# Fifteen gather slots instead of twelve, with memory taken from the descriptor ring and the queries, and two pieces of ScalarE work moved, in a hybrid encoder kernel

## The reference, cut to what matters

```
q = (yt @ w_q).reshape(T, 8, 2, 128)
s = einsum('thpc,pnc->thpn', q, sub_keys)
val, idx = top_k(s, 16)
cand = val[:, :, 0, :, None] + val[:, :, 1, None, :]
top_val, top_pos = top_k(cand.reshape(T, 8, 256), 16)
gate = softmax(top_val)
act = gate * gelu(einsum('thkd,td->thk', u[expert], yt))
out = einsum('thk,thkd->td', act, v[expert])
```

## Time and profile before

| | |
|---|---|
| three runs | 1624.79, 1625.91 (median) and 1631.22 us |
| the profiled execution | 1626.37 us, of which the span of its instructions is 1624.6 us |
| busy share of the span | PE 64%, PEld 44%, DVE 69%, ACT 28%, POOL 31% |
| moved by DMA | 649.84 MB, on average 400 GB/s; 553.68 MB of it by the gathers |

### The profile page before, as it was taken

How to read it: one execution, slowest core, us unless ns; L and a number is a source line. 1 busy time by engine, 2 the same in 40 slices (tenths; PEclk the granted TensorE clock), 3 DMA queues, 4 the chain that set the end, 5 groups by cost and what they waited for, 6 DMA issues and landing times.

```text
span 1624.6 us, 19989 instructions
## 1 busy us (share of the span) xinstructions
PE 1046.7 (64%) x6936; PEld 712.2 (44%) x6936; DVE 1113.1 (69%) x3119; ACT 462.3 (28%) x953; POOL 502.6 (31%) x541
## 2 busy tenths in 40 slices
PE   8996876747644476867573477776576444544454
PEld 8995643525411265756451165655364111211111
DVE  3446768675577765987756765897756777777764
ACT  4101544111011235743121134763222111111110
POOL 0012334322233322333313322332323333333330
PEclk9997868868855799888796579887897566666655
DMA  9969999999999999899999999899999999999994
GB/s 371 355 230 380 417 411 408 419 421 417 418 422 421 421 418 417 352 421 407 420 416 421 421 419 417 353 409 394 415 418 405 422 422 422 421 422 422 421 421 194
DMA packets 106164, 649.84 MB, mean 400 GB/s; under 512 B 11728, under 2 KB 15824, under 8 KB 38480
## 3 DMA queue, kind: packets, MB, share of 16 engines
q0 software_dynamic: 76032, 553.68, 82.4%
q1 hardware_dynamic: 26400, 92.81, 14.7%
q10 hardware_dynamic: 3632, 2.08, 0.4%
HBM read 647.48 MB, written 1.05 MB: 399 GB/s over the span
## 4 chain that ended last, share of the span: by engine, by line
DMA 40%; PE 26%; DVE 16%; POOL 5%; ACT 5%; issue 5%; DVEq 2%; POOLq 0%; ACTq 0%
DMA ring<-in_uv_dram,expert 33%; PE ps L668 13%; DMA wring<-in_wall_dram 8%; DVE ring L1197 7%; PE ps L845 7%; POOL ring L391 5%; ACT side L569 2%; PE ps L858 2%; DVE side L1252 2%; PE ps L675 1%; ACT L460 1%; PE ps L833 1%; DVE picked L1189 1%; DVE mix L1213 1%; PE ps L886 1%
## 5 line engine op out<-in xcount | busy, mean ns | idle before, releaser
L1197 DVE CUSTOM_DVE_ANT_0 ring<-ring,ps 128x1024 f32<-128x1024 f32 x528 | 635.2, 1219 | 321.2 <-DMA ring<-in_uv_dram,expert 250.8
L391 POOL DMA_INDIRECT ring<-in_uv_dram,expert x528 | 500.5, 948 | 1086.6 <-PE ps L845 840.0
L845 PE MATMUL ps<-ring,mix 128*32 128x512 f32 x2112 | 365.6, 827 | 311.4 <-DVE mix L1213 311.2
L845 PEld LDWEIGHTS ps<-ring,mix 128*32 128x32 f32 x2112 | 67.4, 134 | 509.7 <-DVE mix L1213 367.8
L668 PE MATMUL ps<-yT,wring 128*128 128x128 f32 (+1 forms) x1472 | 205.6, 301 | 71.8 <-DMA wring<-in_wall_dram 43.7
L642 ACT ACTIVATE gel<-dots 128x4 f32<-128x4 f32 x132 | 27.1, 205 | 739.2 <-DVE dots L1197 738.8
L668 PEld LDWEIGHTS ps<-yT,wring 128*128 128x128 f32 x1472 | 193.6, 207 | 94.6 <-DMA wring<-in_wall_dram 48.1
L858 PE MATMUL ps<-sel,osb 128*128 128x16 f32 x528 | 84.0, 304 | 78.6 <-ACT osb L628 78.6
L858 PEld LDWEIGHTS ps<-sel,osb 128*128 128x128 f32 x528 | 80.6, 241 | 116.7 <-ACT osb L628 116.7
L569 ACT ACTIVATE side<-ident,params 128x128 f32<-128x128 f32 x310 | 96.5, 389 | 16.0 <-PE ps L886 14.8
L833 PE MATMUL ps<-ident,yg 128*128 128x128 f32 x264 | 49.1, 348 | 71.6 <-DVE dots L1197 71.6
(11 more groups left out here) (207 smaller groups left out, 1043.8 us busy)
## 6 DMA issues: line engine op xcount, KB each, us to landing
wring<-in_wall_dram SPq DMA_DIRECT2D x124, 512.0 KB, 12.2
ring<-in_wall_dram SPq DMA_DIRECT2D x52, 512.0 KB, 13.2
ring<-in_uv_dram,expert POOLq DMA_INDIRECT x528, 16.3
out_dram<-fo ACTq DMA_DIRECT2D x16, 64.0 KB, 6.9
hT<-in_xT_dram ACTq DMA_DIRECT2D x1, 576.0 KB, 15.9
hT<-in_xT_dram SPq DMA_DIRECT2D x2, 256.0 KB, 3.3
params<-in_smalls_dram ACTq DMA_DIRECT2D x1, 380.0 KB, 19.2
params<-in_smalls_dram ACTq DMA_DIRECT2D x1, 50.0 KB, 2.8
```

Of the source, the lines that this page charges most:

```text
L391: pool.indirect_dma_start(out=ring[:, i % R, :], out_offset=None, in_=uv, in_offset=bass.IndirectOffsetOnAxis(ap=expert[:, n % 2, k:k + 1] ...
L845: mm = pe.matmul(po[32 * j:32 * j + 32, half, :], mix[:, k, :], ring[:, slot, D + 512 * half:D + 512 * (half + 1)], start=(q == 0), stop=( ...
L1197: nc.vector.tensor_tensor_reduce(out=row, in0=row, in1=yrep, scale=1.0, scalar=0.0, op0=ALU.mult, op1=ALU.add, accum_out=dots[:, k:k + 1]) ...
```

## The change

- The ring has 15 slots. 12 KB of each partition come from the descriptor ring of POOL's DMAs, which is given 4,096 bytes a partition instead of its default of 16,384; 8 KB come from `qT`, which now holds 9 groups instead of 17 and is filled again for each of three blocks of tokens; 2 KB come from `cand`, `cand2` and `hot`, which share one tile `pairs`.
- Slots are numbered so that gathers 0 to 2 use the three new slots, which nothing else uses: seven gathers, not four, can start before the start-up's weight chunks are used (`FREE = 7`).
- Queries are made later, since `qT` must have been read: `qB` in `u` = 23 to 26 at four chunks a quarter, `q1` in `v` = 23 to 26. Each begins with a wait of ScalarE on `s_sc`.
- The first 20 diagonals of each block are made in `v` = 0; none in `v` = 6.
- `gates(0)` stands after `front(-4)` instead of `front(-1)`.

```
-R = 12
+R = 15
+    def slot(i):
+        return (i + R - 3) % R
+    def query(n):
+        return n - max(b for b in (0, GF, G0, G0 + GA - 1) if b <= n)
     for k in range(16):
-        FRONT.setdefault(21 + min(k // 3, 4), []).append(("qB", k))
+        FRONT.setdefault(23 + k // 4, []).append(("qB", k))
-    FREE = 4
+    FREE = R - 8
-        qT = sb("qT", [P, 2, NG, H, GT])
+        qT = sb("qT", [P, 2, NG - GF, H, GT])
-        cand = sb("cand", [P, TOPK, TOPK])
-        cand2 = sb("cand2", [P, TOPK, TOPK])
+        pairs = sb("pairs", [P, 2, TOPK, TOPK])
-        hot = sb("hot", [P, 2, TOPK, TOPK])
-                    pool.indirect_dma_start(out=ring[:, i % R, :], out_offset=None, in_=uv,
+                    pool.indirect_dma_start(out=ring[:, slot(i), :], out_offset=None, in_=uv,
                     if name == "qB":
                         act.wait_ge(s_proj, m + 1)
-                        act.copy(qT[:, k % 2, GF:NG, k // 2, :], ...
+                        if k == 0:
+                            act.wait_ge(s_sc, GF)
+                        act.copy(qT[:, k % 2, :, k // 2, :], ...
             rows(0)
-            for u in range(-4, 0):
+            front(-4)
+            gates(0)
+            for u in range(-3, 0):
                 front(u)
-            gates(0)
-                if 6 <= v < 14:
-                    for i in range(20 * (v - 6), min(20 * (v - 5), len(TAPS))):
+                if v == 0 or 7 <= v < 14:
+                    u = max(v - 6, 0)
+                    for i in range(NDIAG * u, min(NDIAG * (u + 1), len(TAPS))):
-                if 22 <= v < 26:
-                    for k in range(4 * (v - 22), 4 * (v - 21)):
+                if 23 <= v < 27:
+                    for k in range(4 * (v - 23), 4 * (v - 22)):
                         m = JOB["q1%d" % w, k]
                         act.wait_ge(s_proj, m + 1)
-                        act.copy(qT[:, k % 2, o0 // GT:o0 // GT + 8, k // 2, :],
+                        if k == 0:
+                            act.wait_ge(s_sc, G0 + w * (GA - 1))
+                        act.copy(qT[:, k % 2, 0:8, k // 2, :],
-    nc = _bacc.Bacc("TRN2", target_bir_lowering=False, num_devices=1)
+    nc = _bacc.Bacc("TRN2", target_bir_lowering=False, num_devices=1, dynamic_dma_scratch_size=4096)
```

More of the change, by code:

```diff
@@ L390, in _ @@
                         pool.wait_ge(s_proj, JOB["inB", 2 * (i - FREE) + 1] + 1)
-                    pool.indirect_dma_start(out=ring[:, i % R, :], out_offset=None, in_=uv,
+                    pool.indirect_dma_start(out=ring[:, slot(i), :], out_offset=None, in_=uv,
                                             in_offset=bass.IndirectOffsetOnAxis(ap=expert[:, n % 2, k:k + 1], axis=0)
-                                            ).then_inc(s_g[i % R], 16)
+                                            ).then_inc(s_g[slot(i)], 16)
                 if n == GF - 1:
@@ L517, in front @@
                         act.wait_ge(s_proj, m + 1)
-                        act.copy(qT[:, k % 2, GF:NG, k // 2, :], ps[:, m % 2, 0:TB].rearrange("p (g t) -> p g t", t=GT)
+                        if k == 0:
+                            act.wait_ge(s_sc, GF)
+                        act.copy(qT[:, k % 2, :, k // 2, :], ps[:, m % 2, 0:TB].rearrange("p (g t) -> p g t", t=GT)
                                  ).then_inc(s_bank[m % 2], 1)
@@ L823, in scores @@
                 for s in range(2):
-                    last = pe.matmul(psc[:, s * NK:(s + 1) * NK], qT[:, s, place(n), :, :].rearrange("p h t -> p (h t)"),
+                    last = pe.matmul(psc[:, s * NK:(s + 1) * NK], qT[:, s, query(n), :, :].rearrange("p h t -> p (h t)"),
                                      keysT[:, 2 * layer_of(n) + s, :], start=True, stop=True)
@@ L843, in values @@
                         k = 4 * q + j
-                        slot = (n * TOPK + k) % R
+                        at = slot(n * TOPK + k)
                         mm = pe.matmul(po[32 * j:32 * j + 32, half, :], mix[:, k, :],
-                                       ring[:, slot, D + 512 * half:D + 512 * (half + 1)], start=(q == 0), stop=(q == 3))
+                                       ring[:, at, D + 512 * half:D + 512 * (half + 1)], start=(q == 0), stop=(q == 3))
                         if half == 1:
@@ L1133, in _ @@
             sc = [psc[:, s * NK:(s + 1) * NK] for s in range(2)]
-            c1 = cand[:, :, :].rearrange("p a b -> p (a b)")
-            c2 = cand2[:, :, :].rearrange("p a b -> p (a b)")
+            cand = pairs[:, 0, :, :]
+            c1, c2 = (pairs[:, i, :, :].rearrange("p a b -> p (a b)") for i in range(2))
+            hot = pairs
             def route_best(n):
@@ L1157, in route_pairs @@
                     nc.vector.max_index(idx[:, s, 8:16], val[:, s, 8:16], rest[:, s, :])
-                nc.vector.tensor_tensor(cand[:, :, :], val[:, 0, :].unsqueeze(2).to_broadcast([P, TOPK, TOPK]),
+                nc.vector.tensor_tensor(cand, val[:, 0, :].unsqueeze(2).to_broadcast([P, TOPK, TOPK]),
                                         val[:, 1, :].unsqueeze(1).to_broadcast([P, TOPK, TOPK]), ALU.add)
@@ L1194, in dot @@
                 i = n * TOPK + k
-                dve.wait_ge(s_g[i % R], 16 * (i // R + 1))
-                row = ring[:, i % R, 0:D]
+                dve.wait_ge(s_g[slot(i)], 16 * (i // R + 1))
+                row = ring[:, slot(i), 0:D]
                 nc.vector.tensor_tensor_reduce(out=row, in0=row, in1=yrep, scale=1.0, scalar=0.0, op0=ALU.mult,
```

## The result

| | before | after |
|---|---|---|
| median of four runs each, on one chip | 1625.47 us (1624.79 to 1631.22) | 1613.03 us (1612.94 to 1614.29) |
| ratio, 95% interval | | 0.9921 (0.9906 to 0.9937) |
| span of the profiled execution | 1624.6 us | 1612.5 us |
| VectorE's last `dot` starts, right after the last gather has landed | 1609.08 us | 1598.63 us |

What follows compares the result with a forecast made beforehand. DMA engines bound the kernel from about 120 us, one slow engine setting the end: 1626.4 - 2.0 (slots) + 0.5 (queries) = 1624.9 us, stated as 1624.5 us, no change, since the runs' median lies 0.5 us lower; range 1618 to 1631 us.

Steps and rivals of the forecast that it cites:

- for the straggler it closes only its own idle time: Three added slots: the one late DMA engine regains only its idle time in seven holes, 2 us (bounds 0.4 to 5).
- some 5 us: How far one DMA engine was taken to be behind the fifteen others after a few hundred us.
- rate of 1.2% to 1.7%: How fast one DMA engine falls behind the others: 5 us in 404, over 6 us in 356.
- the straggler isn't one engine: Rival: a different DMA engine is last in each hole, so most of 17.4 us returns; 1615 us, down to 1609; 9%.
- `gates(0)` and diagonals: Start-up and moved diagonals: VectorE's 9.35 us wait goes, 5.96 us of diagonals fit under DMA; nothing added at the end.
- First gathers: Start-up: gathers 4 to 6 skip the weight-chunk wait, filling the hole at 148 to 164 us; counted within the slots' 2 us.
- Queries later: Scores right behind the last query chunks, three times: 0.5 us of loss, between 0.8 us gain and 13 us loss.
- The descriptor ring: POOL's gather issue: smaller ring turns every 14 gathers or so, 0.2 to 1.7 us each, hidden in waits; 0.
- Weights: Slower rival: weight chunks queue behind all gathers, up to +130 us over some 100 chunks; 1640 us or more; 3%.
- neither slower rival: Either POOL waits for all gathers at each ring turn (1660 us and more, 5%), or weight chunks fall behind gathers (3%).

## Why the prediction was wrong, point by point

**What held.** One DMA engine is last, the holes of the fifteen others can be worth nothing to it, and at 652 us they were: taking the start of the `dot` of the same gather in both traces, after is 4.8 to 5.0 us ahead before that hole and 5.0 to 5.1 us behind it. In the kernel after it holds throughout: from 300 us on the last engine is 1.0 us or more behind at every `dot` that waited, and closing the holes of the others (the run with earlier indices) gives next to nothing.

**The step that failed** is "for the straggler it closes only its own idle time", 2 us in all, with 0.4 us for five of the seven holes. It rested on a lag of "some 5 us" that was read at two places and taken for the rest. The lag isn't a standing distance: a hole that outlasts it sets it to 0, and then it takes one fetch of VectorE's instructions after another to come back, at 0.8 us a fetch. A hole costs its length less the lag at that moment. From the trace of before:

| hole | others idle, us | lag ahead of it, us | cost, us | gain measured at the same gathers, us |
|---|---|---|---|---|
| 148 to 164 us | 2.6 | 0.0 | 2.6 | 2.1 |
| 240 us | 0.7 | 0.2 | 0.5 | 2.8, by 500 us |
| 652 us | 5.9 | 4 to 5, still alone at 660 us | 0 | 0.1 |
| 1032 us | 5.4 | 2.3 | 3.1 | 3.4 |
| 1080, 1120 us | 2.0 | 0.0 | 2.0 | 1.8, with 1236 us |
| 1236 us | 0.8 | 1.7, then 0.0 | 0 | |
| sum | 17.4 | | 8.2 | 10.2 |

The row at 240 us fits worst; the next paragraph has a reason. The prediction's own rate of 1.2% to 1.7% contradicts a standing 5 us: in the 48 us between the holes at 1032 and 1080 us it lets a lag of 0.6 to 0.8 us grow. And where the earlier trace rows has single microseconds at 149, 657 and 1038 us, these two of before, within other holes, show more than one engine left, so that no single one had been hiding the hole:

```profile
1122.00:1123.00 1.00, 0.00 (x0) 0.00 (x0) 1.00 (x3) 1.00 (x4) 0.69 (x2) 1.00 0.20 82
1240.00:1241.00 1.00, 1.00 (x10) 0.71 (x6) 0.51 (x2) 0.00 (x0) 0.69 (x2) 1.00 0.47 197
```

**A term that was missing.** The holes were measured by the busy share. After a hole the engines are busy but slower. In the trace of before, behind the hole at 1032 us, a share of 0.99 goes with 383 GB/s, and ten microseconds later 1.01 with 423:

```profile
1040.00:1050.00 10.00, 9.70 (x84) 7.28 (x86) 9.86 (x28) 7.95 (x29) 5.89 (x7) 1.00 0.99 383
1050.00:1060.00 10.00, 9.42 (x82) 6.66 (x74) 9.69 (x33) 7.81 (x28) 3.84 (x4) 1.00 1.01 423
```

By the rate, (1 - GB/s / 421) x length over the seven stretches of the earlier trace rows gives 23.6 us, not 17.4. At 240 us it matters most: from 236 to 260 us the rate is 384 GB/s at a share of 0.97, 2.1 us by the rate, where 0.7 was counted.

```profile
236.00:260.00 24.00, 17.52 (x104) 8.39 (x104) 22.33 (x57) 10.98 (x17) 8.76 (x9) 0.81 0.97 384
```

The work of an engine, on average, falls from 1589.5 to 1585.8 us, 3.7 us. It is 1589 to 1590 us in all three traces with twelve gathers queued and 1585 to 1587 us in those with 14 or 15 and no load added. This is enough for the rest of the 10.45 us beyond 8.2, though how much of it fell to the last engine was not measured.

**The rival** of 1615 us ("the straggler isn't one engine") came within 2 us, in part by luck: its ground was wrong for after, where it is one engine, at the end alone for longer than before, and 1.65 us of the difference are the tail's. What was right in it is that most holes of before cost time, because no single engine was still at work in them. It deserved more than 9%.

**`gates(0)` and diagonals**, each costed at nothing, are together worth 3.8 us by the medians (1.5 us in the traces); how this is split is not shown. For the diagonals the trace has 1.0 us. "Shortens the same holes a second time and adds nothing" was the fault: with 15 slots the diagonals at `v` = 6 still open a hole at 1032 us. Moved to `v` = 0 they cost nothing visible, as predicted. For `gates(0)` the reading held: VectorE's wait of 9.35 us is gone, and it waits for the gelu instead.

```profile
141.92 0.22 DVE L1223 SCALAR_TENSOR_TENSOR coef<-gel,grec,gexp 128x4 f32<-128x4 f32 x1 [7.25 <-ACT gel L656]
```

`values(0, 0)` starts at 142.59 us, and at 144.71 us with both pieces moved back: the 2 us or so that were expected. What this is worth at the end, the runs with both pieces and with the diagonals alone moved back put at 1.3 us by the medians and 1.6 us at the last `dot`; executions of one kernel differ by as much.

**First gathers.** The hole at 148 us is closed (0.85 to 1.01), worth 2.1 us and not hidden, since the lag was still 0. No run had the seven early gathers undone alone.

**Queries later**, 0.5 us of loss: no loss is seen, and the hole at 1236 us is gone (0.91 to 1.02). It wasn't tried by itself. **The descriptor ring**, 0: right (0.9998), but not for the reason given: a turn each 14 gathers shows in no trace. (The prediction's own working gives 28 gathers for 4,096 bytes and then uses 14, without saying why.) **Weights**: a chunk lands in 12.7 us, 12.2 before, though a gather now takes 23.4 us; neither slower rival came about. By the Trainium skill (the same page, "Latency and other measured facts") two fixed engines are usually slower, with the descriptor ring's port as a guess for the cause. The runs agree in part: one engine stays last throughout the kernel after. They show another cause for it, VectorE's instructions. The guess was not tested: a ring of a quarter of the size moves nothing, but the gathers have 76,032 packets with either.

## What to carry to other kernels

A hole in a stream that many engines share costs its length less what the last engine has still to do at that moment; read that lag at each hole, since the hole before may have used it up, and measure the hole by the rate, not by the busy share. When the last engine no longer idles, filling holes gives nothing more; find out what that engine does besides, here fetching VectorE's instructions, and make less of that (more of it cost 11 us here; less of it shows in the profiles, not yet in the medians).

## What the runs showed of the hardware that was not expected

- VectorE's instructions are fetched in packets of 8 KB on the DMA engine that is last here, at about 0.7 to 1.1 us each (8.8 us at the last `dot`, 11.0 us in the medians, for ten). Instructions that cost VectorE nothing visible so cost the whole kernel 9 to 11 us. As many on ScalarE and POOL cost nothing clear of the spread (1.1 and 0.2 us).
- Beside a fetch of VectorE's one gather packet takes 0.96 or 0.97 us instead of 0.31, beside one of ScalarE's or POOL's 0.65 to 0.69 us. Why they differ was not looked for.
- Fully busy DMA engines can be a quarter slower: 322 GB/s against 419 at a share of 1.02, while a chunk of 120 and 8 partitions was loaded, and 383 at 0.99 after a hole. The cause was not looked for.
- The same 16 matmuls at the end took 3.59 us in the execution of before and 1.96 us in that of after, at a granted clock of 0.50 and 1.00.
